# HGRN2 projections of f and q: seven-product units per head in place of dense projections

## What is computed

```python
h = rms_norm(x, norm_w) * (1.0 + scale) + shift
aq, ak, av, ag, rq, rf, ri, rg = split(h @ w_in)
attn = sliding_window_attention(rope(norm(aq)), rope(norm(ak)), av, sinks) * silu(ag)
f = lb + (1.0 - lb) * sigmoid(rf)
rec = rms_norm(hgrn2_chunkwise(rq, f, ri), rec_norm_w) * silu(rg)
out = x + gate * (concatenate([attn, rec], -1) @ w_out)

def hgrn2_chunkwise(q, f, i):            # per chunk of 64 tokens
    b = cumsum(log(f));  b_last = b[-1]
    q_dec, k_inv, k_out = q * exp(b), (1 - f) * exp(-b), (1 - f) * exp(b_last - b)
    o = tril(q_dec @ k_inv.T) @ i  +  q_dec @ S         # S: state before the chunk
    S = exp(b_last) * S + k_out.T @ i
```

## Time and profile before

| | us |
|---|---|
| median of 3 runs | 1863.14 (1861.97 to 1864.21) |
| profiled execution | 1862.2 |
| its span in the trace | 1860.4 |
| PE busy | 1807.2 (97%) |
| DVE busy | 1286.7 (69%) |
| ACT busy | 978.0 (53%) |
| POOL busy | 536.0 (29%) |
| mean granted clock of PE | 0.993 of full |
| moved by DMA | 222.36 MB, 120 GB/s |

### The profile page before, as it was taken

The page is one execution under the profiler, slowest core; times in us unless marked ns, Lnnn a source line. Parts: engine busy times, 40 slices in busy tenths (PEclk is TensorE's granted clock), DMA queues, the critical chain, the costliest instruction groups (busy, mean ns, idle before and its releaser), DMA issues.

```text
span 1860.4 us, 29446 instructions
## 1 busy us (share of the span) xinstructions
PE 1807.2 (97%) x10380; PEld 1513.6 (81%) x10380; DVE 1286.7 (69%) x2612; ACT 978.0 (53%) x2111; POOL 536.0 (29%) x865
## 2 busy tenths in 40 slices
PE   6999999999999999989999999999999999999999
PEld 3788888888878888778888888887788887788887
DVE  6965476777766566677546677776865556977987
ACT  3522225777776665542322577777556555343442
POOL 1000026766733323300002576773333321000000
PEclk9999999999999999989999999999999999999999
DMA  9142332221223344344133222121422238278352
GB/s 366 52 159 88 116 105 94 73 71 45 81 95 97 102 142 125 109 152 158 62 132 108 101 72 76 41 80 57 171 75 78 67 133 292 100 249 285 106 175 91
DMA packets 162081, 222.36 MB, mean 120 GB/s; under 512 B 11792, under 2 KB 104336, under 8 KB 155792
## 3 DMA queue, kind: packets, MB, share of 16 engines
q1 hardware_dynamic: 161936, 220.49, 35.7%
HBM read 163.18 MB, written 57.28 MB: 118 GB/s over the span
## 4 chain that ended last, share of the span: by engine, by line
PE 89%; DMA 3%; DVE 3%; POOL 2%; issue 1%; SPq 1%; ACT 1%; POOLq 0%; DVEq 0%; ACTq 0%
PE bank L847 70%; PE bank L1002 3%; PE bank L991 3%; PE bank L1021 3%; PE bank L1069 2%; PE bank L1054 2%; PE bank L1082 2%; PE bank L1047 1%; PE bank L957 1%; DMA wa<-in_w_ada 1%; PE bank L1071 1%; PE bank L1096 1%; DMA g_raw<-in_w_in 1%; DMA o_lower<-mixed_cols 1%; SPq L487 0%
## 5 line engine op out<-in xcount | busy, mean ns | idle before, releaser
L847 PE MATMUL bank<-h_hi,w_hi 128*128 128x512 f32 x512 | 206.8, 404 | 0.2
L847 PE MATMUL bank<-h_lo,w_hi 128*128 128x512 f32 x512 | 199.9, 390 | 0.0
L847 PE MATMUL bank<-h_hi,w_lo 128*128 128x512 f32 x512 | 199.7, 390 | 0.0
L847 PE MATMUL bank<-ob_hi,oa_hi 128*128 128x512 f32 x448 | 175.8, 393 | 3.7 <-DVE ua L2061 3.7
L847 PE MATMUL bank<-wq_hi,h_hi 128*128 128x384 f32 x512 | 177.6, 347 | 1.7 <-DVE u L1826 1.7
L847 PE MATMUL bank<-ob_hi,oa_lo 128*128 128x512 f32 x448 | 175.0, 391 | 0.0
L847 PE MATMUL bank<-ob_lo,oa_hi 128*128 128x512 f32 x448 | 174.9, 390 | 0.0
L847 PE MATMUL bank<-wq_hi,h_lo 128*128 128x384 f32 x512 | 172.5, 337 | 0.0
L847 PE MATMUL bank<-wq_lo,h_hi 128*128 128x384 f32 x512 | 171.8, 336 | 0.0
L1252 ACT ACTIVATE g_hi<-g_raw 128x2048 fp32r<-128x2048 f32 x36 | 68.9, 1914 | 182.4 <-PE bank L847 159.2
L2313 POOL TENSOR_TENSOR k_out<-b_cum 128x512 f32<-128x512 f32 x32 | 37.4, 1168 | 357.0 <-DVE b_cum L1856 357.0
(11 more groups left out here) (247 smaller groups left out, 4839.2 us busy)
## 6 DMA issues: line engine op xcount, KB each, us to landing
g_raw<-in_w_in SPq DMA_DIRECT2D x24, 1024.0 KB, 6.1
raw<-in_w_in SPq DMA_DIRECT2D x16, 1024.0 KB, 7.8
o_lower<-mixed_cols SPq DMA_DIRECT2D x32, 512.0 KB, 6.1
nat_rows<-u SPq DMA_DIRECT2D x48, 256.0 KB, 2.5
raw<-in_w_in SPq DMA_DIRECT2D x8, 1536.0 KB, 6.5
o_upper<-in_w_out SPq DMA_DIRECT2D x24, 512.0 KB, 8.3
wa<-in_w_ada SPq DMA_DIRECT2D x8, 1024.0 KB, 11.8
g_q<-gate_cols SPq DMA_DIRECT2D x64, 128.0 KB, 2.5
```

The source lines that it names most:

```text
L847: mm = pe.matmul(dst, a, b, start=(first and m == 0), stop=(last and m == 2), **more)
```

## The change

Head 0 is projected as before, from `project_f` and `project_q`. For heads 1 to 7 the two quads of a head are taken together: f and q of both are one product of the segment's h (two token halves by two inner halves) and the head's weights (two inner halves by f and q), and this is computed by seven products of half size in the scheme of the dense stage, in the order P1, P2, P6, P5, P3, P7, P4, each 12 matmuls of 128x512 (4 inner blocks times three split products). f of the first quad is P1 + P2, q of the first quad and q and f of the second are sums of the others, partly accumulated in the banks 0 and 1, partly through SBUF.

- The sums of h (S1, S2, S3, S4, each a high and a low part of 1 MB) are written to DRAM (`sums_d`) in unit 0 of the dense stage, 8 transfers a segment, behind the waits shown. S2 and S1 are read back at the end of the attention, S4 and S3 at the start of the recurrence, on SP behind a wait for q of iteration 1 and ahead of the x blocks (segment 0) or of `gate_bc` and the first gate piece (segment 1).
- A head's weights come in four transfers of 0.26 MB (`rq_raw`), each asked for when the head before has done with its place. Seven operands are made of them: ACT takes the high half (`rec_hi`), DVE the low half (`rec_lo`); `rq_hi` and `rq_lo` have two places, so the split of one product waits for the end of the product two before it. DVE also forms the four sums of weights (`rec_t1_t2`, `rec_t4`, `rec_t3`).
- ACT copies P1, P6 and P5 (with what they have accumulated) out of the banks (`copy_product`); DVE adds (`add_c11`, `add_c12`, `add_c22`). `forget_tanh` of the first quad reads the sum, and `decay_q` reads sums in SBUF.
- The order of all engines' work is written anew per head (`rec_head`, with a = 2h-1 and b = 2h the iterations whose chunk work it carries), with its ends `rec_into_dense` and `rec_into_output`. x blocks have one place `xt`, pieces of `w_ada` are half as large and eight (`gate_piece`), and stand in the DVE order behind `rec_lo(P6)` and behind `rec_lo(P4)`. Squares of x blocks go by whole blocks (`square_next`).
- Into dense stage 1 the first weights and A11 are split within the last head or behind it, in a third place of `g_hi`/`g_lo`; `o_T` has moved, so that ACT's wait for its spill ahead of S1 goes; `gemm_s1` of segment 1 waits for the blocks of P1. The parts of the output stage's operands have other places.

The core of the diff:

```diff
+            def store_sum(s, i, pair):
+                for part, src in enumerate(pair):
+                    sp.dma_start(sums_d[s, i, part], src.bitcast(F32)).then_inc(a21_out, 16)
+            def load_sum(s, i, pair, landed):
+                for part, dst in enumerate(pair):
+                    sp.dma_start(dst.bitcast(F32), sums_d[s, i, part]).then_inc(landed, 16)
...
+                if u == 0:
+                    sp.wait_ge(a21_out, (16 + SUM_STORES) * s + 16)
+                    sp.wait_ge(hop_ok, (PRODS + 1) * s + 3)
+                    store_sum(s, S1, s_pair(S1))
+                    sp.wait_ge(hop_ok, (PRODS + 1) * s + 4)
+                    store_sum(s, S2, s_pair(S2))
                 sp.wait_ge(t4_ok, 2 * n + 2)
                 if not last:
                     sp.wait_ge(wlo_ok, PRODS * n + 4)
                     load_quarter(n + 1, B11)
                     sp.wait_ge(wlo_ok, PRODS * n + 5)
                     load_quarter(n + 1, B12)
+                    if u == 0:
+                        sp.wait_ge(hop_ok, (PRODS + 1) * s + 5)
+                        store_sum(s, 3, s3_pair())
+                        sp.wait_ge(hop_ok, (PRODS + 1) * s + 6)
+                        store_sum(s, S4, s_pair(S4))
...
                         carry(g)
+                    if b == ATT_B - 5:
+                        sp.wait_ge(qkv_ok, S + ATT_B)
+                        load_sum(s, S2, s_pair(S2), xq_in[0])
+                        load_sum(s, S1, s_pair(S1), xq_in[0])
...
+                sp.wait_ge(rq_ok, 2 * (s + 1))
+                load_sum(s, S4, s_pair(S4), xq_in[1])
+                load_sum(s, 3, s3_pair(), xq_in[2])
+                if s + 1 < SEGS:
+                    load_x(0)
+                    load_x(1)
+                else:
                     sp.dma_start(gate_bc[:], b_gate).then_inc(gate_in, 16)
                     load_gate(0)
...
+                for h in range(1, RHEADS):
+                    a, b = 2 * h - 1, 2 * h
+                    last = h + 1 == RHEADS
+                    if h >= 2:
+                        spill(a - 2)
+                        x_slot(h - 1, 2)
+                    value_load(s, b)
+                    if s + 1 < SEGS and last:
+                        load_quarter(GU * (s + 1), B11)
+                    if last:
+                        sp.wait_ge(rprod_ok, rec_prod(s, h, P2))
+                        if s + 1 < SEGS:
+                            sp.wait_ge(xt_out, 16 * 2 * NBLK)
+                            for q, k in enumerate((K1, K2)):
+                                sp.dma_start(h_f[:, k, T1], x_T_d[:, k, T1]).then_inc(xq_in[q], 16)
...
+                    next_head(h, R_B11, rw_lo_ok, rec_prod(s, h, P5))
+                    next_head(h, R_B21, rsum_ok, rec_sum(s, h, 3))
+                    x_slot(h, 0)
+                    if gate_at(s, h, 1) is not None:
+                        load_gate(gate_at(s, h, 1))
+                    gate_load(s, b)
...
+            R_OPERANDS = {P1: A11, P2: A12, P6: in_s(S2), P5: in_s(S1), P3: in_s(S4), P7: A21, P4: A22}
+            def rec_product(s, h, i):
+                V = rec_unit(s, h)
+                pe.wait_ge(rw_lo_ok, rec_prod(s, h, i))
+                if i == P1:
+                    pe.wait_ge(fth_ok, s * REC_T + 2 * h)
+                if i == P2 and h == 1:
+                    pe.wait_ge(qdec_ok, s * REC_T + 2)
+                if i == P6:
+                    pe.wait_ge(rcopy_ok, 3 * V + 1)
+                    if h == 1:
+                        pe.wait_ge(xq_in[0], 80 * s + 64)
+                if i == P5:
+                    pe.wait_ge(radd_ok, 3 * V + 1)
+                if i == P3:
+                    pe.wait_ge(rcopy_ok, 3 * V + 3)
+                    if h == 1:
+                        pe.wait_ge(xq_in[1], 48 * s + 32)
+                if i == P7:
+                    pe.wait_ge(rcopy_ok, 3 * V + 2)
+                    if h == 1:
+                        pe.wait_ge(xq_in[2], 64 * s + 32)
+                if i == P4:
+                    pe.wait_ge(radd_ok, 3 * V + 3)
+                fresh = i in (P1, P2, P5)
+                dst = bank[1 if i in (P2, P5, P3) else 0][:, :]
+                slot = rec_prod(s, h, i) % 2
+                for k in range(KH):
+                    ah, al = R_OPERANDS[i](k)
+                    wh, wl = rq_hi[slot][:, k, :], rq_lo[slot][:, k, :]
+                    mm = split_products(dst, ((wh, ah), (wl, ah), (wh, al)), fresh and k == 0, k == KH - 1,
+                                        skip_group_check=not fresh)
+                mm.then_inc(rprod_ok, 1)
...
+            def rec_head(s, h):
+                a, b = 2 * h - 1, 2 * h
+                rec_product(s, h, P1)
+                output_step(s, b - 2)
+                rec_product(s, h, P2)
+                rec_product(s, h, P6)
+                side_step(s, h, 0)
+                chunk_step(s, a)
+                rec_product(s, h, P5)
+                state_step(s, a)
+                mix_transposes(s, b - 2)
+                rec_product(s, h, P3)
+                output_step(s, a)
+                side_step(s, h, 1)
+                rec_product(s, h, P7)
+                chunk_step(s, b)
+                rec_product(s, h, P4)
+                state_step(s, b)
+                mix_transposes(s, a)
+                side_step(s, h, 2)
+            def rec_into_dense(s):
+                gemm_p1(s + 1, 0, 0)
+                output_step(s, REC_T - 2)
+                gemm_p1(s + 1, 0, 1)
+                mix_transposes(s, REC_T - 2)
+                chunk_step(s, REC_T - 1)
+                gemm_p1(s + 1, 0, 2)
+                state_step(s, REC_T - 1)
+                gemm_p1(s + 1, 0, 3)
+                output_step(s, REC_T - 1)
...
                     act.wait_ge(sums_ok, 4 * s + 1)
-                    for b in range(2):
-                        geq(act, rec_out[b], s * 16 * (REC_T // 2))
                     hi(s_hi[S1][:], s_f[S1][:])
                 weights_hi(n, 2)
...
+            def rec_hi(s, h, i):
+                N = rec_prod(s, h, i)
+                geq(act, rprod_ok, N - 2)
+                if i in (P1, P2, P3):
+                    q = {P1: R_B11, P2: R_B21, P3: R_B22}[i]
+                    act.wait_ge(a_in[q], quarter_landed(s, h))
+                else:
+                    act.wait_ge(rsum_ok, rec_sum(s, h, {P5: 1, P6: 2, P7: 4, P4: 3}[i]))
+                act.activation(rq_hi[N % 2][:], R_SOURCES[i][:], ACT.Copy).then_inc(rw_hi_ok, 1)
+            def copy_product(s, h, i):
+                act.wait_ge(rprod_ok, rec_prod(s, h, i))
+                if i == P6:
+                    act.wait_ge(o_ok, s * REC_T + 2 * h - 1)
+                if i == P5:
+                    act.wait_ge(qdec_ok, s * REC_T + 2 * h)
+                src, dst = {P1: (bank[0], f_even), P6: (bank[0], q_dec[0]), P5: (bank[1], q_odd)}[i]
...
+            def rec_head(s, h):
+                a, b = 2 * h - 1, 2 * h
+                last = h + 1 == RHEADS
+                forget_tanh(s, a)
+                rec_hi(s, h, P2)
+                forget_log(s, a)
+                if h >= 2:
+                    mix_copy(s, a - 2)
+                copy_product(s, h, P1)
+                rec_hi(s, h, P6)
+                chain_end(s, a)
+                rec_hi(s, h, P5)
+                mix_squares(s, b - 2)
+                gate_tanh(s, a)
+                forget_tanh(s, b)
+                copy_product(s, h, P6)
+                rec_hi(s, h, P3)
+                keys_copy(s, a)
+                forget_log(s, b)
+                copy_product(s, h, P5)
+                rec_hi(s, h, P7)
+                chain_end(s, b)
+                mix_copy(s, b - 2)
+                square_next(s, h, True)
+                if last and s + 1 < SEGS:
+                    weights_hi(GU * (s + 1), 0)
+                if last and s + 1 == SEGS:
+                    out_hi(0, 0, 0)
+                rec_hi(s, h, P4)
+                mix_squares(s, a)
+                gate_tanh(s, b)
+                if not last:
+                    rec_hi(s, h + 1, P1)
+                    keys_copy(s, b)
+                    square_next(s, h + 1, False)
+                elif s + 1 < SEGS:
+                    hi_a11(s + 1)
+                    keys_copy(s, b)
+                else:
...
+            def rec_lo(s, h, i):
+                N = rec_prod(s, h, i)
+                dve.wait_ge(rw_hi_ok, N)
+                dve.tensor_tensor(rq_lo[N % 2][:], R_SOURCES[i][:], rq_hi[N % 2][:].bitcast(F32), ALU.subtract
+                                  ).then_inc(rw_lo_ok, 1)
+            def rec_t1_t2(s, h):
+                dve.wait_ge(a_in[R_B12], quarter_landed(s, h))
+                dve.wait_ge(rw_lo_ok, rec_prod(s, h, P1))
+                dve.tensor_tensor(rq_raw[R_B11][:], rq_raw[R_B12][:], rq_raw[R_B11][:], ALU.subtract).then_inc(rsum_ok, 1)
+                dve.wait_ge(a_in[R_B22], quarter_landed(s, h))
```

(57 more changed lines are left out.)

812 lines of the change are left out of this document (440 added, 372 removed).

## The result

The changed kernel takes 1932.56 us (1930.92 to 1935.47, four runs) where the kernel before takes 1862.95 on the same chip: 1.0375 times the time, interval 1.0357 to 1.0393. The forecast was 1906, range 1868 to 1932; the measured time lies 0.6 above the range. Slower was right; of the 69.6 us, 43 were forecast.

A forecast was written before the change was run, and what follows sets the result against it. The prediction took TensorE (PE, busy for 97% of the span) as the bound. Recurrence segments +24.7 and +4.7, clock +4, dense stage +4.6 and seams +5 gave +43 on 1862.2: 1905, 1906 as a median, range 1868 to 1932.

The forecast's parts named there:

- What PE saves: Heads: 12 matmuls fewer save 2.73 us, less 2 x 0.18; net 2.4 a head, 33 us in 14 heads.
- The first head: Recurrence start: loads behind S4 and S3 make P1 start at 22.3 us, not 8.9 (segment 0); P2 waits 9.3 (segment 1).
- rival (3): First head: x and gate loads are not held up by S4 and S3; -15.5 and -4 for the clock, 1886; 13%.
- The clock: PE at half rate behind the two long first-head gaps, 2 us each: +4, from 0 to 8.
- The heads: Recurrence heads: new waits on PE eat the gain; 34.5 us a head in segment 0, 32.3 in segment 1.
- rival (4): Heads: DVE operations slowed beside POOL, +10 us, with slow writes +8 more; 1917 to 1930; 15%.
- if DVE ran without any of its splits and sums the segments would still be only 18 us shorter: Recurrence segments: a bound of the walk on what DVE's splits and sums cost, 18 us for each segment.
- The dense stage: Stores of sums delay the c22 blocks; DVE waits some 7 us, PE 2.3, twice: +4.6, from 0 to 12.
- The seams: Ends of the recurrence: into dense stage 1 +5 us; into the output stage 0, from -3 to +5.
- (1): Whole kernel: PE stays the bound, splits, sums and hand-overs lie in its shadow, first loads land in time; 1830; 7%.
- (2): Recurrence: steady heads gain with waits below 0.5 us, first loads cost; 1865 to 1875, or 1855; 10%.
- The likely case itself: Whole kernel: the walked forecast holds, 1890 to 1917 us; 53%.

The follow-up runs named there:

- x_first: The changed kernel with the first x blocks, or gate_bc and the first gate piece, issued ahead of the S4 and S3 loads; 1917.7 us.
- dve_sums_seams: sums_on_dve_2 with the new orders of both seams and the early load of A21; 1851.75 us, 0.9935, the fastest kernel.
- less_dve: The changed kernel with three of DVE's four sums of weights per head made over one column only (wrong output); 1925.0 us.
- all_three: The changed kernel with x and gate loads issued earlier, S3 and S4 stored later, and DVE's order within a head changed; 1892.3 us.
- best_2: heads_2 plus new seam orders (1860.0), with A21 loaded early, a first-weights split of dense 1 on POOL, mix transposes behind P3; 1858.3 us.
- sums_on_dve_2: heads_2 with the four sums of weights back on DVE, everything else the same; 1868.0 us, 1.0017.
- stores_later: The changed kernel with S3 and S4 stored in the second unit of the dense stage, behind its c11 blocks; 1922.0 us.
- heads_2: all_three with the four sums of weights on POOL and new orders of DVE and ACT in the heads; 1869.8 us, 1.0035.

## Why the prediction was right or wrong

Of the 69.6 us, 43 were forecast. The spans are 28.4 further apart than forecast: 11.9 at the output seam, where nothing was forecast, 6.1 in the recurrence of segment 1, 6.1 in the two dense stages, 2.8 in the recurrence of segment 0 and 2.5 at the seam into dense 1, less 1.0 in the attention. The step that failed is the first of these: the seam into the output stage was put at nothing.

**What PE saves** (12 x 0.228 less 2 x 0.18 a head): right. The instructions are 168 fewer. Head 6 of segment 1 takes 32.87 us, and the gaps in its timeline add up to 2.95, so 29.9 without, where two iterations took 32.3 with none: 2.4 us, as forecast.

**The first head**: right. 22.1 for 22.3 us from q to P1, 8.8 for 9.3 at P2 in segment 1, and x_first with the order of issue alone takes the gap of segment 0 down to 2.6. The price of rival (3), -15.5 and -4 for the clock, is 19.5; x_first gave 14.9, and its trace still has a stretch of half clock behind P2 in both segments. What I left out is that P2 of segment 0 waits another 2.15 for q_dec. The late x block does not make this wait: with the block in time it is 2.15 and 2.05 in dve_sums_seams, where tanh, Ln, scan, Exp and decay_q of iteration 1 follow one another and PE has only P1 and the outputs to do meanwhile.

**The clock**: the price of a place was right (1.6 to 1.9 us for 2), their number was not. P1 behind the 13.2 us gap took 4.9 us for 3.0, the window's granted clock was 0.50 in it, and P2 behind the 8.8 in segment 1 took 4.75. But gaps of 2.2 us in the heads did it too (below), and the new gaps in the dense stages and at the seams: the trace has twelve stretches with matmuls of 0.63 us, where it had three. Two more were forecast, nine came. They hold 58 more such matmuls, each 0.20 us apart more than at full rate (steps of 0.43 and 0.23), which makes 12 us by this estimate, in place of 4. These 12 us are part of the stretches of the table.

```profile
569.00:573.00 4.00, 3.65 (x9) 2.91 (x10) 3.06 (x8) 2.73 (x4) 0.92 (x3) 0.50 0.00 0
```

**The heads**: the mechanism was right and the size off. Behind the first, the six heads of segment 0 last 35.1 us each from P1 (605.88 to 816.4; 34.5 forecast) and those of segment 1 33.1 (1394.7 to 1593.45; 32.3 forecast): 6 x 0.6 + 6 x 0.8 = 8.4 us, of the 8.9 by which the two segments lie above the forecast. In segment 0 the excess is the clock's: P1 at 712.73 and P4 at 811.94 run at half rate and cost 1.6 us each; without these 3.2 us its heads last 34.6, as walked. Segment 1 has no such fall behind its first head. There head 4, the one of the walk, takes 34.3 us for 32.9, with waits of 3.5 (0.72, 0.57, 1.28, 0.97) for 2.8. The mis-sized term in it is DVE's: a low half of 512 columns was taken as 0.6 and an own sum as 0.6; the lines of DVE by form show

```profile
L1991 DVE TENSOR_TENSOR rq_lo<-rq_raw,rq_hi 128x512 fp32r<-128x512 f32 x70 | 53.9, 770 | 24.2 <-ACT rq_hi L1484 24.2
...
L1991 DVE TENSOR_TENSOR rq_lo<-rq_t,rq_hi 128x512 fp32r<-128x512 f32 x28 | 29.0, 1036 | 23.8 <-ACT rq_hi L1484 23.8
...
L1997 DVE TENSOR_TENSOR rq_raw<-rq_raw 128x512 f32<-128x512 f32 x14 | 9.7, 692 | 1.5
```

Seven splits take (53.9 + 29.0) / 14 = 5.9 us a head instead of 4.2, four sums 2.7 instead of 2.4: 2.0 us more. In less_dve 1.6 us of DVE work less a head made segment 1 5.05 us shorter, 0.45 per us; by this estimate the 2.0 are worth 0.9 a head, which is the 0.8 of segment 1. That segment 0 came out as walked in spite of them means that another term was too large there; which one stays open, and the agreement is partly luck.

A split is longer where it lies beside POOL's work. The same 28 splits of `rq_t`, 1.04 us in the mean above, take 0.68 in dve_sums_seams, whose order puts them elsewhere (there the fourth sum is the stretched one, 1.00 for 0.68):

```profile
L1993 DVE TENSOR_TENSOR rq_lo<-rq_t,rq_hi 128x512 fp32r<-128x512 f32 x28 | 18.9, 675 | 0.0
```

That is rival (4), and a timeline of all_three shows its mechanism, DVE and then POOL:

```profile
1503.80 0.68 DVE L2006 TENSOR_TENSOR rq_raw<-rq_raw 128x512 f32<-128x512 f32 x1
1505.54 2.62 DVE L2272 SCALAR_TENSOR_TENSOR s_in<-s_in,e_b,bank 128x128 f32<-128x128 f32 x7
1508.46 1.11 DVE L1990 TENSOR_TENSOR rq_lo<-rq_raw,rq_hi 128x512 fp32r<-128x512 f32 x1
1509.49 1.77 DVE L2399 SCALAR_TENSOR_TENSOR rg_w<-o_sq,rg_w 128x512 f32<-128x512 f32 x1
```

```profile
1507.75 1.27 POOL L2656 TENSOR_TENSOR k_inv<-k_f,k_inv 128x512 f32<-128x512 f32 x1 [1.01 <-ACT k_inv L1526]
1508.98 1.73 POOL L2658 TENSOR_TENSOR k_out<-k_f,k_out 128x512 f32<-128x512 f32 x1
```

With both operands in SBUF a sum takes 0.68 while POOL rests; beside POOL a split takes 1.11 and rg_w 1.77 (0.68 in the earlier trace rows), and POOL's own goes from 1.27 to 1.73; the carries, one operand of which is in PSUM, take 2.62 with POOL's subtraction beside them, as they took 2.65 in the earlier trace rows. The Trainium skill, "SBUF — State Buffer", section on who interferes with whom, says just this: a DVE instruction contends with GpSimd's reads when both its inputs are in SBUF, and not with at most one, as long as it is outside the 2-port perf modes. The operations that POOL held up in best_2 (6.19 us for 1.91) have one tensor from SBUF; whether they run in such a mode no run here shows. What a head pays for it isn't measured apart from the order.

**The bound "if DVE ran without any of its splits and sums the segments would still be only 18 us shorter"** stood against the pure theory of load, and less_dve bears it out (7.6 of 22 us). But the forecast took the order of the diff for the only one: the orders tried later, with the same work, are worth 21 us more in the two segments (sums_on_dve_2 against all_three).

**The dense stage** is a mis-sized term: DVE waited 9.6 us for 7, PE 2.9 and 5.7 for 2.3 each. The mechanism is what stores_later shows. Behind each of PE's waits stands a stretch of half clock too. That PE waits twice as long in dense 1 is not the queue's doing: the last store lands 16.3 and 16.1 us after its issue, the four blocks of c after 12.8 and 12.7, and DVE waits 9.6 and 10.5. DVE's wait is 0.9 longer, and PE runs out of work 1.9 us sooner behind it; why it has less to do there stays open.

**The seams**: into dense 1, +5 was walked and +7.5 came. Into the output stage, "as much work on both sides: 0" is the step that failed, the largest miss with 11.9 us. The work is as much; the chain is not where it was. I counted what stands on both sides and did not walk the chain of iteration 15 from the end of P4, as I had done at the other seam. The edits of the seams and the early A21, on top of the new heads, take all of it back: 12.2 in sums_on_dve_2 becomes 0.6 in dve_sums_seams.

**The rivals**: (1) had the matmuls right and every wait wrong. (2) has the heads as another order gives them (29.2 to 33.0 us behind the first in dve_sums_seams), but its price for the first head is gone there too, with the loads issued ahead. (3) fell. (4) holds in kind, and the time lies 2.6 us above even its range. The likely case itself had its mechanisms right in all terms but that of the output seam, yet nearly all erred to the same side: gaps were not followed by a fall of the clock except in two places, and DVE's instructions had durations that nothing beside them had slowed.

**What stays open**: the 1 to 2 us that dense 0 still shows in some of the kernels; and why dve_sums_seams keeps its waits of 0.4 to 1.8 us a head. They and the matmuls fit together: 16.5 us a segment saved by PE, less 7.8 and 9.7 of waits, and 8.2 and 7.0 measured. That DVE, at 93%, now sets them is likely, but argued, not shown.

## What to carry to other kernels

A product scheme that takes matmuls off a bound engine has also to be paid in latency: walk every chain that runs through the recombined outputs (above all the last one at each seam, where no other product hides it) before counting the matmuls saved. In a kernel whose engines take their work in a fixed order, the order of the same work and transfers decided 81 us (1932.6 to 1851.8), taking 22 us of DVE's work away 8 (less_dve), and moving it to another engine nothing. Small loads that the next step needs are to be issued ahead of large ones that have time, stores of a few MB behind those whose buffers come next.

## What the hardware showed that I had not expected

**The granted clock falls behind some gaps of 2.2 us and not behind others.** Behind an idle time of 2.15 us at 578.29 P2 ran at full rate (3.00 us). Behind 2.22 at 712.73, in the middle of the segment's heads, P1 took 4.57: its rows go to 0.63 from the third matmul on.

```profile
713.03 0.40 PE L927 MATMUL bank<-h_hi,rq_lo 128*128 128x512 f32 x1
...
713.63 0.63 PE L927 MATMUL bank<-h_hi,rq_hi 128*128 128x512 f32 x1
```

In the heads it never fell behind 0.9 to 1.3 us. In x_first P1 behind 2.59 stays at full rate and P2 behind 2.76 drops with its first row. In dve_sums_seams P2 behind 2.15 stays and P2 behind 2.05 drops. So the length of a gap alone doesn't say it, and a wait slightly over 2 us can cost 1.6 us more than its length. What decides it no run here shows.

**Moving a sum off a busy DVE gained nothing.** Four sums a head on POOL (heads_2, 1869.8) and on DVE (sums_on_dve_2, 1868.0) are within the measurement, though DVE is the busier engine by far. A large split moved to POOL (best_2) even held up DVE's own work beside it, by 4.3 us.
